# Sparse attention's gate projection: features as output rows, x as the moving operand, then turned; the sigmoid issued later

## The reference

```python
proj = h @ w_in                                   # h: 256 tokens x 1024, w_in: 1024 x 2608
q = proj[..., :1024]; kv = proj[..., 1024:2560]   # 16 heads; six k/v parts of 256 columns
gates = jax.nn.sigmoid(proj[..., 2560:].reshape(B, S, 16, 3))   # 48 columns: 16 heads x 3 paths
...
o = gb[..., 0:1] * o_cmp + gb[..., 1:2] * o_slc + gb[..., 2:3] * o_win
```

## Time and profile before

| | us |
|---|---|
| median of 3 runs | 1497.08 |
| the profiled execution, whole | 1496.34 |
| its span in the trace | 1494.4 |
| TensorE busy | 1434.9 |
| VectorE busy | 781.1 |
| ScalarE busy | 638.4 |

### The profile page before, as it was taken

How to read it: one execution, slowest core, us unless ns; L and a number is a source line. 1 busy time by engine, 2 the same in 40 slices (tenths; PEclk the granted TensorE clock), 3 DMA queues, 4 the chain that set the end, 5 groups by cost and what they waited for, 6 DMA issues and landing times.

```text
span 1494.4 us, 24718 instructions
## 1 busy us (share of the span) xinstructions
PE 1434.9 (96%) x10418; PEld 1278.5 (86%) x10418; DVE 781.1 (52%) x1207; ACT 638.4 (43%) x1105; POOL 176.7 (12%) x149
## 2 busy tenths in 40 slices
PE   9999999999899899999899999899999979998998
PEld 8989999999755699999888876788888869878998
DVE  6876555546546665654623356433233363574554
ACT  5645444443355554445432344433232243454452
POOL 0010211001200011110004000021111002201110
PEclk9999999999999999999999999999999989999999
DMA  8435655454487445554331310222223213314553
GB/s 309 139 122 178 212 184 181 172 184 145 167 287 265 154 170 191 177 188 151 113 114 57 102 57 1 83 86 98 100 85 112 86 53 116 132 57 141 177 191 113
DMA packets 56974, 211.16 MB, mean 141 GB/s; under 512 B 6176, under 2 KB 9888, under 8 KB 53536
## 3 DMA queue, kind: packets, MB, share of 16 engines
q1 hardware_dynamic: 56128, 206.40, 40.2%
q10 hardware_dynamic: 736, 3.18, 0.6%
HBM read 208.51 MB, written 1.05 MB: 140 GB/s over the span
## 4 chain that ended last, share of the span: by engine, by line
PE 89%; DVE 5%; ACT 3%; DMA 1%; POOL 1%; issue 1%; SPq 0%; ACTq 0%; POOLq 0%; DVEq 0%
PE psum L299 24%; PE psum L300 23%; PE psum L301 23%; PE psum L1153 2%; PE psum L1174 2%; DVE WL L232 2%; PE psum L1307 2%; PE psum L298 2%; PE psum L297 2%; PE psum L296 2%; PE psum L2177 1%; PE psum L1463 1%; PE psum L1157 1%; PE psum L445 1%; ACT WH L227 1%
## 5 line engine op out<-in xcount | busy, mean ns | idle before, releaser
L299 PE MATMUL psum<-XH,WH 128*128 128x256 f32 (+1 forms) x2048 | 638.1, 312 | 13.5 <-DVE WL L232 8.5
L300 PE MATMUL psum<-XL,WH 128*128 128x256 f32 (+1 forms) x2048 | 630.4, 308 | 0.0
L301 PE MATMUL psum<-XH,WL 128*128 128x256 f32 (+1 forms) x2048 | 629.6, 307 | 0.0
L232 DVE TENSOR_TENSOR WL<-stage,WH 128x1024 fp32r<-128x1024 f32 x334 | 397.9, 1232 | 319.7 <-ACT WH L227 319.5
L227 ACT ACTIVATE WH<-stage 128x1024 fp32r<-128x1024 f32 x334 | 335.1, 1051 | 363.6 <-PE psum L301 323.7
L299 PEld LDWEIGHTS psum<-XH,WH 128*128 128x128 f32 x2048 | 396.1, 193 | 41.5 <-issue 17.5
L300 PEld LDWEIGHTS psum<-XL,WH 128*128 128x128 f32 x2048 | 396.7, 194 | 16.8 <-issue 0.5
L301 PEld LDWEIGHTS psum<-XH,WL 128*128 128x128 f32 x2048 | 396.6, 194 | 16.8
L2333 POOL TENSOR_TENSOR arena<-arena,con 128x512 f32<-128x512 f32 (+1 forms) x48 | 51.4, 1070 | 400.3 <-DVE con L2264 399.7
L1265 ACT ACTIVATE arena<-psum,SM 128x16 f32<-128x16 f32 (+3 forms) x144 | 67.4, 478 | 25.9 <-DVE SM L1201 11.8
L1250 ACT ACTIVATE arena<-psum 128x512 f32<-128x512 f32 (+2 forms) x48 | 35.4, 737 | 79.8 <-PE psum L1174 79.6
(11 more groups left out here) (255 smaller groups left out, 1700.3 us busy)
## 6 DMA issues: line engine op xcount, KB each, us to landing
stage<-w SPq DMA_DIRECT2D x132, 512.0 KB, 4.5
stage<-merge SPq DMA_DIRECT2D x80, 512.0 KB, 4.6
ring<-ada SPq DMA_DIRECT2D x24, 1024.0 KB, 5.2
stage<-in SPq DMA_DIRECT2D x44, 512.0 KB, 4.7
stage<-ab_in SPq DMA_DIRECT2D x24, 512.0 KB, 4.9
stage<-nsa_in SPq DMA_DIRECT2D x20, 512.0 KB, 4.8
stage<-out SPq DMA_DIRECT2D x16, 512.0 KB, 4.6
stage<-ab_out SPq DMA_DIRECT2D x8, 512.0 KB, 4.2
```

Source lines behind the costliest of these rows:

```text
L232: e.tensor_tensor(lo, raw, hi.bitcast(F32), ALU.subtract).then_inc(s_lo, 1)
L299: e.matmul(dst, wh, xh, start=start, stop=False)
L300: e.matmul(dst, wh, xl, start=False, stop=False)
L301: return e.matmul(dst, wl, xh, start=False, stop=stop)
```

## The change

The gates' weights become the stationary operand (128 x 64) and x the moving one (128 x 256), so that the result has 64 rows (features) and 256 columns (tokens), in 8 x 3 matmuls. VectorE copies it from psum to `N.tmp` between the `low` of `n.kc` and that of `n.vc`. TensorE then turns it with two matmuls against the identity, after `n.kc` and ahead of `n.vc`, into a bank of its own, `n.turned.gates`. ScalarE does one more `high` (that of `n.ks`) ahead of `inverse_scalar` and one more (`n.kw`) after it; then it waits for `n.turned.gates` and takes the sigmoid, and two `high` instead of four follow. The count of `high_next` is the same, 11.

```diff
@@ nsa_tensor
             w = Chunk(flow, "nsa_gates", 0)
             b = tile(e, "n.gates")
-            for t in range(2):
-                x = (lambda k: e.wait_ge(*ve.of(f"nn.x{k}"))) if t == 0 else None
-                rows(e, b[:, t * 64:(t + 1) * 64], w, t, slice(0, 64), "n.gates", x, 256)
+            for k in range(8):
+                e.wait_ge(*ve.of(f"nn.x{k}"))
+                t = product(e, b[0:64, 0:256], w, k, slice(0, 64), XH[:, k, CTX], XL[:, k, CTX], k == 0, k == 7)
+            t.then_inc(*pe.tick("n.gates"))
             w.done()
             fm(4, "n.kc")
+            b = tile(e, "n.turned.gates")
+            e.wait_ge(*ve.of("n.gates"))
+            for t in range(2):
+                i = e.matmul(b[:, t * 64:t * 64 + 64], N.tmp[0:64, 0, t * 128:t * 128 + 128], ident[0:64, 0:64], start=True,
+                             stop=True)
+            i.then_inc(*pe.tick("n.turned.gates"))
             fm(5, "n.vc")
@@ nsa_vector
             low_next(e, flow)
+            e.wait_ge(*pe.of("n.gates"))
+            e.tensor_copy(N.tmp[0:64, 0, :], banks["n.gates"][0:64, 0:256]).then_inc(*ve.tick("n.gates"))
+            banks.emptied("n.gates", ve)
             low_next(e, flow)
             next(rms)
             next(rms)
@@ nsa_scalar
+            for _ in range(3):
+                high_next(e, flow)
+            inverse_scalar(e, "nn")
             high_next(e, flow)
-            high_next(e, flow)
-            inverse_scalar(e, "nn")
+            e.wait_ge(*pe.of("n.turned.gates"))
             for t in range(2):
-                e.activation(N.gt[:, t, :], banks["n.gates"][:, t * 64:t * 64 + 48], ACT.Sigmoid,
+                e.activation(N.gt[:, t, :], banks["n.turned.gates"][:, t * 64:t * 64 + 48], ACT.Sigmoid,
                              scale=narrow("nn", 1)[:, t:t + 1]).then_inc(*ac.tick("n.gates"))
-            banks.emptied("n.gates", ac)
-            for c in range(4):
+            banks.emptied("n.turned.gates", ac)
+            for c in range(2):
                 high_next(e, flow)
```

## The result

The changed kernel took 1490.78 us (median of 7 runs, 1486.53 to 1492.68), the kernel before, on the same chip, 1497.48 us (7 runs, 1495.90 to 1499.23): a ratio of 0.9949, interval 0.9935 to 0.9963. It is faster by 6.7 us on the medians and, over all runs of both kernels with a clock on record, by 7.7 us in the means, where 4.9 us were forecast. The profile finds 4.6 us at the places where the forecast had put 4.9. The rest of the gain goes with less low clock elsewhere, which the forecast did not count.

A forecast was written before the change was run, and what follows sets the result against it. TensorE bounds the kernel (89% of the chain). 1.29 + 1.22 - 0.4 + 1.86 = 3.97, and 0.94, make 4.9 us: 1496.34 to 1491.4 on the profiled execution, 1492.2 on the median; range 1490.0 to 1495.6.

The forecast's parts named there:

- The gates' product: Gates: 24 matmuls at 0.120 us end at 324.5, not 327.3; `n.kc` waits for `WL`, so 1.29 us saved.
- The slow clock at the gates: First half of `n.kc`: without 64-column matmuls no fall to half clock, 2.96 us instead of 4.18, saving 1.22.
- the first rival: Behind the gates: clock falls all the same, TensorE idling 1.5 us; 3.4 us saved in all, 1493.7; chance 0.15.
- the other side: Clock falls in the gap at 324.5, stays low through `n.kc` and `n.vc`: 5.3 us slower, 1502.4; chance 0.04.
- The turning: Two fp32 matmuls on TensorE's path ahead of `n.vc`: costs 0.4 us, between nothing and 0.61.
- The stall: TensorE's wait for `WL` between `n.vc` and `n.ks` goes as the sigmoid moves later: 1.86 us saved.
- VectorE's copy: Copy of 64 x 256 from psum between two `low`: at most 0.43 us, nothing waits, cost nothing.
- The bank: At `y0.0.0`, about 952 us: one more result shifts later psum banks, ending a wait for ScalarE's read; 0.94 us saved.
- the clock's term: First half of `n.kc` at full clock, 2.96 us instead of 4.18: 1.22 us saved.
- everything ... moves as a block: From 344 to 952 and after 953 us, work is released by engines finishing, not wall time, so it shifts together.
- given back in the attention: At 405 to 500 us, a low-clock stretch some 3 us longer costs up to 3 us: 1495.2; chance 0.12.
- luck: Lower end of the range, 1490.0: turning at nothing and favourable low-clock stretches elsewhere.

The follow-up runs named there:

- the wide version: Kernel before with the sigmoid moved and the gates' product as 48 matmuls of 256 columns instead of 64: 1490.04 us, ratio 0.9953.
- setting the circle back: Changed kernel with the psum bank rotation moved on by seven after `n.ready`, so later results take their old banks: 1494.28 us, ratio 0.9973.
- setting it on alone: Kernel before with only the psum bank rotation moved on by one after `n.ready`: 1496.34 us, ratio 0.9985.
- The added matmuls: Overwritten 256-column matmuls ahead of `n.ks`: 8, 16, 24 in the changed kernel, 1489.27, 1491.81, 1488.95 us; 8, 16 in the kernel before, 1499.42, 1497.20 us.
- the changed kernel with 24 added: Changed kernel with 24 matmuls of 256 columns (2.88 us) ahead of `n.ks`, their result overwritten: 1488.95 us, ratio 0.9950.

## Where the prediction was right, and the step that failed

- *The gates' product:* forecast 0.120 us a matmul, measured 0.1135. It didn't matter, for `n.kc` waited for its `WL` as forecast: it starts 4.40 us after the gates and not 5.68, saved 1.28 (forecast 1.29). About 0.4 us of the 1.28 is clock: without the slow last steps the narrow product takes 5.28 us.
- *The slow clock at the gates:* `n.kc`'s first half took 3.03 us and not 4.18, saved 1.15 (forecast 1.22). The clock did not fall in or behind the gap of 1.5 us, in any of the seven profiles that have it, so the first rival fell, and with it the other side. (In the stretch that the rival was drawn from, the burst behind the gap of 2.53 us began at the full clock, and the fall came about 0.9 us into it.) That the narrow matmuls are what goes ahead of the fall is borne out by the wide version; what it is about them stays open.
- *The turning:* from the sums to the inverse 7.97 us against 7.28, 0.69 lost, of which 0.59 are the turning's own rows; forecast 0.4, and the whole is just above its upper bound of 0.61. Of the other 0.1, 0.07 stands between the mean and the turning (333.36 to 333.79, where the mean and the next product are 0.36 apart before).
- *The stall:* from the inverse to `n.ks` 3.32 us against 5.18, saved 1.86 (forecast 1.86). Without the later sigmoid it comes back. `n.kw` and `n.vs` were not late.
- *VectorE's copy:* 0.41 us between the two `low`, at no cost, as forecast.
- *The bank:* 1.02 us (forecast 0.94), shown from both sides, by setting the circle back and by setting it on alone.
- *The sum:* 3.60 + 1.02 = 4.62 us in the profiles, against 4.9. The missing 0.3 is the turning. The parts without the clock were forecast at 4.9 - 1.2 = 3.7, and 3.7 is what the runs give at equal clock, but that is in part luck: in the profiles these parts are 0.9 (the gates' product less its slow steps) - 0.7 + 1.9 + 1.0 = 3.1.

The step that failed is the clock's term: "Saved: 1.22", together with "everything ... moves as a block". It was read from one execution, as a fixed property of one place, and was mis-sized: by the slope over all runs the clock's part of the gain is about 4.0 us on average (6.1 us less lost clock at 0.66), not 1.2. Two things were off. The low stretch at the gates lasts 3.4 us in some executions of the kernel before and 6.8 in others; with the slow steps of the gates' product it cost about 1.6 us in the first kind (1.15 + 0.4) and 3.1 in the second (1.48 more). The profile that I read was of the cheaper kind, and its execution was itself 1.1 us under the median of the first seven runs. And low stretches elsewhere did not stay as they were: from 1211 to 1262 us the first pair of profiles shows 1.03 us gained where only the clock differs, and near 787 us other versions gained 3.4 us in the same way. I had put changes of low stretches elsewhere down as a loss ("given back in the attention") and as "luck" at the lower end; they were a large part of the gain. In the profile of the attention itself, 405 to 500 us, nothing was given back (3.33 us ahead at 394, 3.35 at 506).

What stays open: why the changed kernel loses 6.1 us less clock, of which the gates account for 1.7 to 3.4 (half of 3.4 or 6.8 us). The versions without narrow matmuls lose 18.1 to 23.9 us on average, those with them 23.1 to 26.4. The added matmuls speak against the mere shift as the reason: one and two microseconds later, the kernel before gains 0.7 us at most, and the changed kernel with 24 added reaches `n.ks` only 0.73 us earlier than before (21.59 against 22.32 us locally) and still loses only 18.1 us. A shift to earlier without the change was not tried. Whether the low stretches near 787 and 1215 us hang on the exact time at which they are reached, or on what the executions' start leaves them, no run here separates.

## What to carry to other kernels

Look at the step of a narrow product before counting on its few columns: here a quarter of the columns saved 7% of a step, and the narrow matmuls were followed by a low clock; fewer matmuls (weights stationary, tokens moving), or even the same number at full width, were better. Look for what sits between two weight splits in an engine's order and can wait, here a table load and a sigmoid: moving it was half of the local gain, for free. And before reading a median for an edit of under 3 us, read the edit in the trace against a ruler of unchanged operations; setting the runs to equal lost clock helps too, to a microsecond or two. Take the clock's term from several profiled executions, over the whole program, not from one place in one.

## What the runs showed of the hardware

- At the full clock, 48 matmuls of 256 columns took 5.75 us and 48 of 64 columns 5.28 us, both with a 128-wide weight load; with a 64-wide load, 256 columns took 0.1135 us a step.
- The granted clock fell to 0.50 during or behind the narrow ones in all seven profiles that have them and in none of the nine others, though TensorE was busy all the time in both the narrow and the wide version. What it is about them stays open.
- The same program had 3.4 us or 6.8 us of low clock at one place, and the runs of one version spread over 3 to 9 us. On average 1 us of lost clock went with 0.66 us of time, but not evenly: 3.4 us of it cost 3.4 us where TensorE was busy throughout (787 to 795 us) and 1.03 us where it idled in part (1211 to 1262 us).
- A table load of 1.28 us was followed by its ACTIVATE 0.02 us later (342.96 + 1.28 to 344.26).
- Two fp32 matmuls of 64 x 64 against the identity took 0.59 us from their first row to the next product, as long as five matmuls of 256 columns.
